# Decoder step on one Trainium2 core: TensorE's small attention products in two groups per step, the values' products at the head of the next step

## The reference, cut to what matters

```
s = einsum('nqhgd,nqkhd->nqhgk', q, kg) * scale + bias        # bias: -slope * distance
m = max(s); lse = m + log(sum(exp(s - m))); p = exp(s - lse)
o = einsum('nqhgk,nqkhd->nqhgd', p, vg)                       # per branch
wts = softmax(stack(lses)); out = sum(wts * stack(outs))      # branches merged, then @ w_o
```

## Time and profile before

| | |
|---|---|
| median of 3 runs | 2574.61 us (2572.23 to 2575.18) |
| the profiled execution's own time | 2574.76 us |
| its span in the trace | 2573.0 us |
| mean granted TensorE clock | 0.995 |
| PE busy over the span | 2518.5 us (98%), 21708 products |
| DVE, ACT, POOL busy | 1587.2, 944.0, 503.0 us (62%, 37%, 20%) |
| the 26 steps of the attention loop | from 1543 to about 1819 us |

### The profile page before, as it was taken

The page is one execution under the profiler, slowest core; times in us unless marked ns, Lnnn a source line. Parts: engine busy times, 40 slices in busy tenths (PEclk is TensorE's granted clock), DMA queues, the critical chain, the costliest instruction groups (busy, mean ns, idle before and its releaser), DMA issues.

```text
span 2573.0 us, 51247 instructions
## 1 busy us (share of the span) xinstructions
PE 2518.5 (98%) x21708; PEld 2407.6 (94%) x21708; DVE 1587.2 (62%) x3133; ACT 944.0 (37%) x2011; POOL 503.0 (20%) x447
## 2 busy tenths in 40 slices
PE   8999999998899999999999999999999999999998
PEld 7899999997899999999999998786999999999997
DVE  6778777777773655655564625657745555555545
ACT  5545444445450322232223414446513223222322
POOL 0111101112100343414330000004103432343200
PEclk9999999999999999999999999999999999999999
DMA  3111111135510211111112324325111111111111
GB/s 148 59 52 44 35 35 44 52 132 177 193 50 25 66 50 50 50 50 50 50 34 75 103 90 129 116 84 179 63 42 58 49 51 44 48 51 52 48 42 66
DMA packets 90316, 182.31 MB, mean 71 GB/s; under 512 B 21985, under 2 KB 54425, under 8 KB 89753
## 3 DMA queue, kind: packets, MB, share of 16 engines
q1 hardware_dynamic: 81081, 166.78, 20.4%
q10 hardware_dynamic: 9008, 12.26, 1.5%
HBM read 147.98 MB, written 36.27 MB: 72 GB/s over the span
## 4 chain that ended last, share of the span: by engine, by line
PE 84%; DVE 8%; ACT 3%; issue 1%; POOL 1%; DMA 1%; ACTq 0%; DVEq 0%; POOLq 0%; SPq 0%
PE psum L2964 7%; PE psum L2963 7%; PE psum L2962 7%; PE psum L2991 6%; PE psum L2992 6%; PE psum L2993 6%; PE psum L2544 5%; PE psum L2545 5%; PE psum L2546 5%; PE psum L2618 4%; PE psum L2619 3%; PE psum L2620 3%; PE psum L2570 2%; PE psum L2807 2%; PE psum L3081 2%; PE psum L3082 1%
## 5 line engine op out<-in xcount | busy, mean ns | idle before, releaser
L2991 PE MATMUL psum<-c_hi,d_hi 128*128 128x258 f32 x1344 | 380.4, 283 | 3.1 <-DVE x L2141 1.7
L2992 PE MATMUL psum<-c_lo,d_hi 128*128 128x258 f32 x1344 | 379.9, 283 | 0.0
L2993 PE MATMUL psum<-c_hi,d_lo 128*128 128x258 f32 x1344 | 379.7, 282 | 0.0
L1368 POOL TENSOR_TENSOR d_lo<-d_raw,d_hi 128x1024 fp32r<-128x1024 f32 x96 | 207.0, 2179 | 609.1 <-ACT d_hi L1139 609.1
L2618 PE MATMUL psum<-x_hi,w_hi 128*128 128x352 f32 (+1 forms) x768 | 272.7, 355 | 2.4 <-DVE pre L1600 2.4
L2991 PEld LDWEIGHTS psum<-c_hi,d_hi 128*128 128x128 f32 x1344 | 254.3, 189 | 4.1 <-DVE x L2141 2.1
L2993 PEld LDWEIGHTS psum<-c_hi,d_lo 128*128 128x128 f32 x1344 | 254.3, 189 | 0.0
L2992 PEld LDWEIGHTS psum<-c_lo,d_hi 128*128 128x128 f32 x1344 | 253.9, 189 | 0.0
L2964 PE MATMUL psum<-x_hi,t_lo 128*128 128x258 f32 x896 | 253.5, 283 | 0.0
L2964 PE MATMUL psum<-x_hi_b,t_lo 128*128 128x258 f32 x896 | 253.5, 283 | 0.0
L2962 PE MATMUL psum<-x_hi,t_hi 128*128 128x258 f32 x896 | 252.8, 282 | 0.0
(11 more groups left out here) (429 smaller groups left out, 6692.7 us busy)
## 6 DMA issues: line engine op xcount, KB each, us to landing
w_raw<-in_w SPq DMA_DIRECT2D x86, 512.0 KB, 3.9
t_raw<-in_w_up SPq DMA_DIRECT2D x56, 512.0 KB, 3.5
d_raw<-in_w_quad SPq DMA_DIRECT2D x48, 512.0 KB, 3.6
q_tile<-scratch_q SPq DMA_DIRECT2D x24, 256.0 KB, 3.4
scratch_att<-o_out ACTq DMA_DIRECT2D x32, 132.0 KB, 2.9
x<-in_x SPq DMA_DIRECT2D x8, 516.0 KB, 9.5
s_state<-in_s_rec_in SPq DMA_DIRECT2D x2, 2048.0 KB, 13.0
out_s_rec<-s_state SPq DMA_DIRECT2D x8, 512.0 KB, 5.4
```

The costliest lines, as they stand in the source:

```text
L1368: pool.tensor_tensor(d_lo[:, d % 3, part], d_raw[:, d % 3, part], f(d_hi[:, d % 2, part]), ALU.subtract).then_inc(sem("quad_ready"), L.add ...
L2991: mm(out, whi, uhi, start=p in (1, 5, 2) and kk == 0, stop=False, skip_group_check=True)
L2992: mm(out, whi, ulo, start=False, stop=False, skip_group_check=True)
L2993: done = mm(out, wlo, uhi, start=False, stop=kk == 1, skip_group_check=True)
```

## The change

Only TensorE's program changes. A moves from the end of its step to the head of the next one, in front of T0. F(3s) moves in front of Tout, so that Tout stands directly in front of T1. S0 follows T1 directly in all steps, and F(3s+1) comes behind it, directly in front of F(3s+2). In step 0, S0 of tile 1 comes ahead of F(1) and F(2). The order of a plain step becomes A of tile s-2, T0, S1, F(3s), Tout, T1, S0, F(3s+1), F(3s+2). No instruction is added or removed on any engine, and the programs of DVE, ACT, POOL and SP stay as they are.

```
@@ -3210,6 +3210,8 @@
                 if step == 0:
                     fill(0)
                     scores(nxt, 0)
+                if step > 1:
+                    apply(tile_of(step - 2))
                 if cur:
                     turn(cur, 0, "q_tile_free" if step == 1 else None)
                 if step == 15:
@@ -3217,10 +3219,10 @@
                     transposes(5, late_values(0, 3))
                 if nxt:
                     scores(nxt, 1)
+                if step:
+                    fill(3 * step)
                 if step > 1:
                     outputs_turn(step)
-                if step:
-                    fill(3 * step)
                 if step == 17:
                     samples_turn()
                 if step == 18:
@@ -3234,18 +3236,13 @@
                 if step == 18:
                     pe.wait_ge(sem("kv_ready"), L.next("kv_ready"))
                     transposes(5, late_values(3, 6))
-                if step < 18:
-                    fill(3 * step + 1)
                 if step < 23:
                     scores(tile_of(step + 1), 0)
-                if step >= 18:
-                    fill(3 * step + 1)
                 if step == 14:
                     samples_rows()
                 if step == 15:
                     samples_scores()
-                if cur:
-                    apply(cur)
+                fill(3 * step + 1)
                 fill(3 * step + 2)
```

## The result

The changed kernel takes 2583.2 us, the median of 8 runs (2582.12 to 2586.17), against 2573.1 us (2571.39 to 2575.18) for the kernel before: a ratio of 1.0035 [1.0026, 1.0044], which is 9.0 us more (6.7 to 11.3); the two medians by themselves lie 10.1 us apart. The same kernel measured a second time gave 1.0027 [1.0018, 1.0036], 7.0 us more (4.6 to 9.3). The forecast was +4.8 us, and its likeliest outcome (0.53) was no change that a measurement can tell, up to 2579.8 us; the kernel is slower than that, by one and a half to two times the forecast, inside the range given.

The account below looks back on a forecast made before the run. TensorE, busy nearly all of the span, was taken as the bound. Plain steps 3.7, step 1 0.1, step 0 1.5, step 8 -0.5 made +4.8 us on 2574.76, so 2579.4 us; range 2575.5 to 2585.5.

Parts of the forecast that it names:

- the plain steps: Steps 2 to 17: 10.85 us each against 10.62, 0.23 more per step, 3.7 us over 16 steps.
- the 0.18: Plain steps: four transposes take 0.53 us in front of S, 0.35 before a fill; T1 now pays this too.
- step 8: S1's wait of 0.46 us for DVE, which was building bias tables, goes: -0.5 us.
- steps 19 to 21: Within steps 18 to 21, which have no fills: order around the loop unchanged, waits stay, 0.
- Step 0: S0 of tile 1 waits about 1.2 us for DVE and runs slower at half clock: +1.5 us, bounds +0.4 and +2.5.
- Steps 22 to 25: Changes of shape stay at six; what longer transposes save, T0 behind A gives back: 0.
- rival 2: S0 waits for DVE's reading of S1 where DVE has more to do: six steps at 1 us, 2585.4; chance 0.15.
- SP at 0: SP's query load waits for T1, which moves less than a microsecond; the tile is wanted a step later: 0.
- Rival 1: The clock falls in longer groups of small products: five groups at 1.5 us, +7.5, 2586.9 us; chance 0.12.
- Rival 3: Only entering and leaving fills costs, and TensorE's two waits go too: -6.3 us, 2568.5 us; chance 0.07.

Follow-up runs that it names:

- experiment 5: The kernel before with S0 directly behind T1 in steps 1 to 17, A and Tout where they were: 2576.43 us, ratio 1.0009.
- experiment 4: The kernel before with step 0 alone in the changed order: 2576.09 us, ratio 1.0005.
- Experiment 2: The changed kernel with steps 18 to 25 back in the order of before: 2580.78 us, ratio 1.0029 to the kernel before.
- experiment 1: The changed kernel with step 0 alone back in the order of before: 2580.87 us, ratio 1.0027 to the kernel before.
- after again: The changed kernel, unchanged, measured and profiled a second time: 2582.54 us, ratio 1.0027 to the kernel before.
- experiments 8 and 9: 8: the kernel before with groups {S1, A, T0}, {T1, S0, Tout} in steps 2 to 17, 2584.27 us; 9: also DVE's program in that order, 2574.45 us.
- experiment 3: The changed kernel with step 0 and steps 18 to 25 in the order of before: 2576.87 us, ratio 1.0013 to the kernel before.

## Why the prediction was right in the plain steps and short in the sum

**Right: the plain steps.** The forecast was 10.85 us per step and +3.7 in sixteen; measured 10.82 and 0.20 x 16 = +3.2. T1 running into S0 pays the 0.18, shown by experiment 5. The sum came from pieces of an existing timeline, each with its own neighbours, and none of them was off by more than 0.01 us. The rule of the Trainium skill, TensorEngine Tiling (Array Packing), Key Properties, that a change of the tiling mode drains TensorE, has the right sign too; counted at one price for all joints it gave +1.8 for these steps where 3.2 were measured.

**Right: step 8** (its wait is gone; S of that step shows no bracket). Neither reason given for it is enough by itself: with A alone moved 0.30 us of the 0.46 stayed, with S0 alone 0.26, and with Tout alone, which the text didn't name, it was gone. **Right: steps 19 to 21** (26.71 against 26.68 us).

**Step 0: right in mechanism, too small.** Forecast +1.5 with bounds of 0.4 and 2.5, measured +2.3. The wait (1.26) and the slow S0 (0.46 more) were as forecast. The term that failed is the stay at half clock. The +1.5 adds the wait, the slow S0 and two joints, and so leaves as many fill products at half clock as before. Those were ten (1552.74 to 1555.6); after, they were sixteen (1555.08 to 1559.93), each 0.13 longer than at full clock, which is the missing 0.8. With the old order the granted clock near step 0 fell for 3.4 us or not at all: step 0 took 9.70 to 9.72 us in five traces and 8.16 or 8.17 in four. With the new order it fell in all five, and in four of them for 6.8 us (11.91 to 12.06; the fifth, experiment 4, 3.4 us and 10.74). On the mean of these traces the order of step 0 costs 11.74 - 9.02 = 2.7 us. That the bound of +2.5 named this case does not make it a forecast.

**Steps 22 to 25: the step that was missed.** The text costed them at 0 by counting joints, and the joints are indeed worth nothing (1.64 measured, 1.70 accounted for by two stops). What it did not do there is what it did for S0: ask how long DVE needs for the bank and what covers that. A between the two output fills was that cover, 1.87 us of it. It was a new wait of the kind of rival 2, on another line and in other steps than rival 2 named. Experiment 2 shows it: without the new order there, the 1.6 us are gone from the trace.

**Rival 2 in step 15: there, and small in the changed kernel.** The rival named a late DMA in step 15. S0 of tile 16 waited 0.30 and 0.97 us in the two executions of the changed kernel, and 0.55, 1.92 and 1.27 in experiments 1 to 3. The text put SP at 0. SP's rows in the changed kernel:

```profile
1707.98 0.33 SPq L621 DMA_DIRECT2D scratch_q<-q_stage  x1
...
1710.80 0.64 SPq L686 DMA_DIRECT2D s_high<-in_s_keys  x1
```

Before, they stand at 1701.62 and 1705.10. The key load is 5.70 us later, while DVE's copy of T0 ahead of it is 4.61 later (1713.00 against 1708.39): 1.1 us of slack are gone. In SP's queue it stands behind the store L621, 6.36 later, of a projection product whose fill now comes behind S0. Not only whose signal SP waits for had to be costed, but also what it stores. The query load, next in that queue, was late for S0 near 1745 in two traces of the new order (0.43 in experiment 1, 0.95 in after again). It was late once in each of experiments 8 and 9 too (0.20 and 0.47), and in neither trace of the kernel before.

**Rival 1: not in the changed kernel.** From 1562.5 to 1743 the granted clock is 1.00 in it, through groups of 3.9 and 4.9 us of small products. It fell in one trace of fourteen (experiment 2), behind a wait of 1.92 us. So a long group alone was not enough in any trace here. The one fall stood behind a long wait and in front of the sample products; experiment 3 has the same group behind 1.27 us of waiting and no fall. One case doesn't show a cause. **Rival 3**, that the saved group is worth something, fell: the saved group cost nothing before, since transposes alone between two fills run at 0.35 for four, and TensorE's two waits stayed.

**Not shown to come from the change:** the 2.0 us behind the loop. In the profiled execution of the changed kernel the clock was at half in two stretches there that the kernel before ran at 1.00:

```profile
1846.80:1850.00 3.20, 3.20 (x14) 3.20 (x13) 2.57 (x6) 1.90 (x3) 0.00 (x0) 0.50 0.47 164
2003.80:2007.00 3.20, 3.20 (x17) 3.20 (x16) 2.99 (x5) 0.00 (x0) 0.00 (x0) 0.50 0.00 0
```

The changed kernel again took 1.3 us less there, with the second of the two falls but not the first. Two variants that keep its new step 0 took 753.41 and 753.64, as little as any kernel, and experiment 4, near the kernel before, took 755.60, with a fall near 1996; neither trace of the kernel before has one there. It is not settled whether a changed order makes these falls more frequent. Without them the parts add up to 7.4 and 8.6 us, against 9.0 (6.7 to 11.3) and 7.0 (4.6 to 9.3) measured. Against the forecast of +4.8 that is 0.2 to 1.5 more in steps 1 to 18, 0.8 in step 0 and 1.6 in steps 22 to 24.

## What to carry to other kernels

Price a reordering on TensorE joint by joint from its own timeline, start to start: here merging three groups into two removed a group that cost nothing (transposes between fills) and made a joint that cost 0.18 us. Then, for each piece that moves, ask of every bank it stood in front of or behind how long the engine that empties it needs in its own fixed order; one A less between two fills cost 1.6 us, and an order of TensorE that its consumer doesn't follow cost 9. (When two traces are compared, look first whether the clock was at half equally long in both: here that alone moved a row by 1.6 us.) An order that moves on one engine has to move on those that take its results, or be left.

## What was not expected of the hardware

- The same program loses a different time to the clock in each execution. Near step 0 the old order showed two cases 1.5 us apart (8.16 without a fall in four traces, 9.70 with one of 3.4 us in five), and the new order, with a wait of 1.26 us right behind one of 1.17, a fall in every one of five, of 6.8 us in four. Why one of them was short, and why four of the old order had none, stays open.
- A bracketed wait costs more than the bracket: 0.95 us in it, but 1.27 - 0.16 = 1.11 from start to start, and the next product 0.11 late as well, 1.22 in all.
- The costs of three edits are not additive: 0.22 + 0.16 + 0.05 us per step alone, 0.20 together.
